# Beginning of a fused decoder step: input rows first, conditioning vectors and nine short rows on ScalarE's queue, the first conditioning weights ahead of two weight blocks

## What is computed

```python
mod = jax.nn.silu(c) @ w_ada + b_ada                       # c: 9 vectors, one for the prompt, 8 for the samples
sh1, sc1, g1, sh2, sc2, g2 = split(mod, 6)
h = rmsnorm(x, norm_mix_w) * (1.0 + sc1) + sh1
z = h @ w_in + b_in                                        # split into q, f, i, og, glu_a, glu_b, gate_a, gate_b
```

## Time and profile before

| | us |
|---|---|
| median of 3 runs | 1910.36 (1909.33 to 1912.45) |
| profiled execution, its own time | 1907.86 |
| its span in the profile | 1906.1 |
| TensorE busy | 1874.0, 98% of the span |
| VectorE / ScalarE / GpSimd busy | 1412.5 / 674.3 / 231.5 |

### The profile page before, as it was taken

How to read it: one execution, slowest core, us unless ns; L and a number is a source line. 1 busy time by engine, 2 the same in 40 slices (tenths; PEclk the granted TensorE clock), 3 DMA queues, 4 the chain that set the end, 5 groups by cost and what they waited for, 6 DMA issues and landing times.

```text
span 1906.1 us, 38795 instructions
## 1 busy us (share of the span) xinstructions
PE 1874.0 (98%) x15832; PEld 1820.0 (95%) x15832; DVE 1412.5 (74%) x2068; ACT 674.3 (35%) x1175; POOL 231.5 (12%) x301
## 2 busy tenths in 40 slices
PE   7999999999999999999999999999999999999998
PEld 6999999999999999998999999999999999999998
DVE  6797979787878888797676666566469988985653
ACT  4322313141322313232454433333445444443432
POOL 5500000000000000000002357476000000000000
PEclk8999999999999999999999999999999999999999
DMA  9722132323130413223277644554542333327653
GB/s 285 225 64 68 46 106 57 105 58 106 50 101 25 125 37 82 80 75 96 74 247 227 193 131 138 165 164 142 153 128 85 94 100 108 94 71 217 194 166 109
DMA packets 382010, 228.22 MB, mean 120 GB/s; under 512 B 17479, under 2 KB 375015, under 8 KB 381824
## 3 DMA queue, kind: packets, MB, share of 16 engines
q1 hardware_dynamic: 381424, 225.11, 40.3%
q10 hardware_dynamic: 416, 0.72, 0.1%
HBM read 195.69 MB, written 30.96 MB: 119 GB/s over the span
## 4 chain that ended last, share of the span: by engine, by line
PE 90%; DVE 5%; DMA 2%; ACT 1%; SPq 1%; issue 1%; POOL 0%; ACTq 0%; DVEq 0%; POOLq 0%
PE Z L1092 36%; PE Z L1074 28%; PE Z L1379 5%; PE Z L1380 5%; PE Z L1381 5%; PE R L1113 2%; DVE w_lo L1557 1%; PE Z L1037 1%; PE R L1169 1%; DMA w_raw<-in_w_out_dram 1%; PE R L1119 1%; ACT w_hi L2253 1%; PE R L1195 1%; PE R L1202 1%; PE R L1176 1%; PE R L1204 1%
## 5 line engine op out<-in xcount | busy, mean ns | idle before, releaser
L1092 PE MATMUL Z<-h_hi,w_hi 128*128 128x352 f32 x1488 | 499.2, 336 | 2.3 <-issue 2.3
L1092 PE MATMUL Z<-h_hi,w_lo 128*128 128x352 f32 x1488 | 478.1, 321 | 0.0
L1092 PE MATMUL Z<-h_lo,w_hi 128*128 128x352 f32 x1488 | 477.6, 321 | 0.0
L2253 ACT ACTIVATE w_hi<-w_raw 128x1024 fp32r<-128x1024 f32 (+1 forms) x227 | 235.0, 1035 | 673.4 <-PE Z L1092 360.8
L1557 DVE TENSOR_TENSOR w_lo<-w_raw,w_hi 128x1024 fp32r<-128x1024 f32 (+1 forms) x225 | 285.0, 1267 | 228.7 <-ACT w_hi L2253 220.0
L1706 DVE SCALAR_TENSOR_TENSOR yb<-up,vec,yb 128x1024 f32 (+1 forms) x240 | 308.3, 1285 | 28.9 <-DVE yb L1706 4.6
L1092 PEld LDWEIGHTS Z<-h_hi,w_hi 128*128 128x128 f32 x1488 | 279.5, 188 | 16.2 <-issue 14.1
L1092 PEld LDWEIGHTS Z<-h_lo,w_hi 128*128 128x128 f32 x1488 | 280.3, 188 | 0.5 <-issue 0.5
L1092 PEld LDWEIGHTS Z<-h_hi,w_lo 128*128 128x128 f32 x1488 | 279.2, 188 | 0.0
L1074 PE MATMUL Z<-act_hi,w_hi 128*128 128x352 f32 x528 | 171.8, 325 | 0.1
L1379 PE MATMUL Z<-h_hi,q_hi 128*128 128x352 f32 x528 | 171.0, 324 | 0.0
(11 more groups left out here) (365 smaller groups left out, 3422.0 us busy)
## 6 DMA issues: line engine op xcount, KB each, us to landing
w_raw<-in_w_in_dram SPq DMA_DIRECT2D x64, 512.0 KB, 5.9
w_raw<-in_w_out_dram SPq DMA_DIRECT2D x48, 512.0 KB, 4.3
w_raw<-in_w_ffn_out_dram SPq DMA_DIRECT2D x47, 512.0 KB, 4.3
w_raw<-in_w_ffn_in_dram SPq DMA_DIRECT2D x44, 512.0 KB, 3.8
raw_a<-in_w_ffn_in_dram SPq DMA_DIRECT2D x88, 256.0 KB, 2.9
aw<-in_w_ada_dram SPq DMA_DIRECT2D x32, 512.0 KB, 5.2
w_raw<-in_w_ffn_out_dram SPq DMA_DIRECT2D x24, 384.0 KB, 3.5
ada_w<-in_w_ada_dram SPq DMA_DIRECT2D x16, 512.0 KB, 7.1
```

The costliest lines, as they stand in the source:

```text
L1092: last = mm(out, w[:, kt, :], x[:, kt, cols], start=kt == 0 and m == 0, stop=kt == NJ - 1 and m == 2)
L2253: A(w_hi[b.par][:, 0:n, :], w_raw[b.par][:, 0:n, :], ACT.Copy).then_inc(w_hi_ready, 1)
```

## The change

SP issues all nine x tiles first, then three of the twelve short rows (norm_mix_w, b_ada, lb_logits), then w_ada for j = 0, the two weight blocks, and the rest of w_ada. The two DMAs of the conditioning vectors and the other nine short rows are issued by ScalarE, the nine one by one behind its nine Squares. The multiply of the conditioning vectors goes from VectorE to GpSimd; the low part of block 1 goes from GpSimd to VectorE, between `scale_prompt(0)` and `prompt_low(0)`; the low part of block 0 goes behind all reciprocal roots on GpSimd. The roots' rows are copied in three pieces of up to four tiles, in place of nine. `vectors()` goes behind the last root row, `conditioning(1)` stands right behind `fold_groups(0)`, `fold_groups(1)` is inside the first step, and the steps of the first products run through kt in order for both blocks to the end.

```diff
-FIRST_STEPS = tuple((kt, b) for kt in range(NJ - 2) for b in range(2)) + tuple(
-    (kt, b) for b in range(2) for kt in range(NJ - 2, NJ))
+FIRST_STEPS = tuple((kt, b) for kt in range(NJ) for b in range(2))
+COND_AFTER = {**{(kt, 0): kt + 2 for kt in range(NJ - 3)}, (NJ - 4, 1): NJ - 1}
+FOLD_WITHIN = {(0, 0): 1, **{(kt, 1): kt + 2 for kt in range(NJ - 3)}}
+FOLD_AFTER = {(NJ - 3, 0): NJ - 1}
+ROWS_A_BANK = 4
+N_ROW_COPIES = (NC + ROWS_A_BANK) // ROWS_A_BANK
...
-            sp.dma_start(crow[0:1, :], c_prompt).then_inc(c_loaded, 16)
-            sp.dma_start(crow[1:NSEQ, :], c_sample).then_inc(c_loaded, 16)
...
-            for t in range(4):
+            for t in range(NC + 1):
                 load_x(t)
...
+            load_rows(sp, V_MIX, 0, norm_mix_w[0].rearrange("(r c) -> r c", c=P))
+            load_rows(sp, 0, 1, b_ada[0].rearrange("(r c) -> r c", c=P))
+            load_rows(sp, V_LB0 - NVA, 1, lb_logits.rearrange("l (r c) -> (l r) c", c=P))
...
-            for t in range(4, 6):
-                load_x(t)
+            load_mod(0)
             for b in range(2):
                 load_first(b)
-            for t in range(6, NC + 1):
-                load_x(t)
-            for j in range(NJ):
+            for j in range(1, NJ):
                 load_mod(j)
...
-                    if t == 2:
-                        vectors()
+                    if t == 4:
+                        conditions()
                 for t in range(NC - 1, NC + 1):
                     root_row(t)
+                vectors()
                 pe.wait_ge(const_ready, 3)
-                for j in range(2):
-                    conditioning(j)
-                    fold_groups(j)
+                conditioning(0)
+                fold_groups(0)
+                conditioning(1)
...
-                        if b == 1 and m == 1 and kt + 2 < NJ:
-                            fold_groups(kt + 2)
+                        if m == 1 and (kt, b) in FOLD_WITHIN:
+                            fold_groups(FOLD_WITHIN[kt, b])
                     if kt == NJ - 1:
                         last.then_inc(block_done, 1)
-                    if b == 0 and kt + 2 < NJ:
-                        conditioning(kt + 2)
+                    if (kt, b) in FOLD_AFTER:
+                        fold_groups(FOLD_AFTER[kt, b])
+                    if (kt, b) in COND_AFTER:
+                        conditioning(COND_AFTER[kt, b])
...
             for j in range(NJ):
                 condition(j)
                 scale_prompt(j)
+                if j == 0:
+                    dve.wait_ge(w_split, 1)
+                    low(Idx(1))
                 prompt_low(j)
...
+            act.dma_start(crow[0:1, :], c_prompt).then_inc(c_loaded, 16)
+            act.dma_start(crow[1:NSEQ, :], c_sample).then_inc(c_loaded, 16)
             act.wait_ge(c_loaded, 32)
...
-
-                if t == 5:
-                    for b in range(2):
-                        hi(Idx(b))
+                load_rows(act, *late_rows[t])
             groups_out(0)
+            for b in range(2):
+                hi(Idx(b))
...
+            pool.wait_ge(c_loaded, 32)
+            pool.wait_ge(csig_ready, 1)
+            st.tell(Q.tensor_tensor(crow[:, :], crow[:, :], csig[:, :], ALU.mult), c_ready, 1)
             for t in range(NC + 1):
                 m = tokens(t)
-                if t == 6:
-                    for b in range(2):
-                        low(Idx(b))
...
+            low(Idx(0))
```

More of the change, by code:

```diff
@@ L545, in store_last, with load_rows @@
             eng.dma_start(y_sample.rearrange("s t d -> (s t) d")[:, cols], yout(c)[n:m, cols]).then_inc(y_stored[hf], 16)
+    def load_rows(eng, row, tile, src):
+        eng.dma_start(vrow[row:row + src.shape[0], tile, :], src).then_inc(rows_loaded, 16)
     def rec7(n):
@@ L958, in _, with conditions @@
             pe.wait_ge(const_ready, 2)
[L960 to L963, removed]
+            def conditions():
+                pe.wait_ge(c_ready, 1)
+                for j in range(NJ):
+                    last = transpose(R[0][:, j * NSEQ:(j + 1) * NSEQ], crow[:, j * P:(j + 1) * P], ident[0:NSEQ, 0:NSEQ])
+                last.then_inc(p0_done, 1)
             def vectors():
@@ L1499, in lower_bounds, with copy_rows @@
                 st.do(V.tensor_scalar(lbs[:, 2, :], lbs[:, 0, :], 1.0, None, ALU.subtract))
-            def copy_row(t):
-                dve.wait_ge(row_made, t + 1)
-                st.tell(V.tensor_copy(rsrow[:, t * P:t * P + tokens(t)], row_bank(t)), row_copied, t + 1)
+            def copy_rows(n):
+                first, end = n * ROWS_A_BANK, min((n + 1) * ROWS_A_BANK, NC + 1)
+                cols = sum(tokens(t) for t in range(first, end))
+                dve.wait_ge(row_made, end)
+                st.tell(V.tensor_copy(rsrow[:, first * P:first * P + cols], Z[1][:, n, 0:cols]), row_copied, n + 1)
             def condition(j):
@@ L1520, in _ @@
                         "p (j t) -> p j t", j=4)), x_evac, n + 1)
-                if t >= 2:
-                    copy_row(t - 2)
-                if t == 3:
-                    first_evac(1, vec[:, :], R[1][:, 0:NVEC])
-            for t in range(NC - 1, NC + 1):
-                copy_row(t)
+                if t == 5:
+                    first_evac(0, ct[:, :, 0:NSEQ], R[0][:, 0:NJ * NSEQ].rearrange("p (j s) -> p j s", s=NSEQ))
+                if t == 6:
+                    copy_rows(0)
+            for n in range(1, N_ROW_COPIES):
+                copy_rows(n)
+            first_evac(1, vec[:, :], R[1][:, 0:NVEC])
             def scale_prompt(j):
@@ L1540, in prompt_low, with low @@
                     st.do(ins) if n == 0 else st.tell(ins, h_ready, j + 1)
+            def low(b, n=8):
+                dve.wait_ge(w_hi_ready, b.v + 1)
+                st.tell(V.tensor_tensor(w_lo[b.par][:, 0:n, :], w_raw[b.par][:, 0:n, :],
+                                        w_hi[b.par][:, 0:n, :].bitcast(F32), ALU.subtract), w_split, b.v + 1)
             for j in range(NJ):
```

33 lines of the change are left out of this document (10 added, 23 removed).

## The result

| | before | after |
|---|---|---|
| median in the same comparison, 12 runs each | 1910.07 (1908.06 to 1912.51) | 1913.92 (1910.12 to 1918.02) |
| ratio to before, 95% interval | | 1.0023 [1.0016, 1.0030] |
| profiled execution, its own time | 1907.86 | 1917.03 |
| its span | 1906.1 | 1915.3 |
| first 352-column matmul, T0 | 32.40 | 36.15 |

The change makes the kernel slower by 3.85 us, 0.23%. That lies above the range given. By the rivals, the time sits between the third and the fourth, and the mechanism is the fourth's.

A forecast was written before the change was run, and what follows sets the result against it. TensorE, 90% of the last-ending chain, was taken as the bound, its head held back by the DMA stream. First 352-column matmul -1.3, from there to block 2 +0.6: -0.7 from 1910.36 gives 1909.7 us, range 1905.6 to 1912.9.

The forecast's parts named there:

- the third: Rival 3, chance 0.15: row issues on ScalarE stand between the Squares, first 352-column matmul at 33.6, +1.8 us, 1912.2.
- the fourth: Rival, chance 0.08: last short row waits behind SP's queued megabytes, lands at 25.9, first 352-column matmul 37.7, +5.9, 1916.3.
- The landing of the last short row: Last row on ScalarE's queue: issued at 16.3, landing taken as 3.0 us, short rows complete at 19.3 (17.6 to 26).
- From the landing to the copy-out: Transposes, copy and conditioning(0) after the short rows: 1.6 + 1.5 + 0.7 for the low clock, copy-out's end at 23.1.
- From the copy-out to T0: Rounding, GpSimd's low part, xs and samples(0): 6.8 us plus 1.2 for VectorE's subtraction, 8.0, ending at 31.1.
- held up by it: scale_prompt operations on VectorE could delay, or be delayed by, GpSimd's low part of block 0; delaying it: up to 1.5 later.
- The sign it gave for GpSimd: On GpSimd's timeline, xs or a first sample operation takes about 1.2 us longer than before.
- Issues on ScalarE: Nine row issues of 0.3 to 0.6 us run during the Squares and cost nothing; ninth Square begins at 15.7.
- From T0 to B2: First 352-column matmul to start of block 2, the steady part: 37.6 us before, small parts together +0.6.
- The wait of 1.65: TensorE's wait at 65.57 for VectorE's last h_lo goes; the copy-out before fold 7 may hold 0.3: -1.35.
- The new wait at B2: Start of block 2: both first blocks now end together, so TensorE waits 2.6 - 1.46 = +1.15 us.
- -2.7 and +1: Ends for the clock between first 352-column matmul and block 2: taken as 0; -2.7 if high all the way.

## Why the prediction was wrong

- **The landing of the last short row.** The step that failed is the one that took 3.0 us for it, "nearer to the small transfer: it is 62 KB, on a queue that has nothing else". It took 6.72, from 16.82 (forecast 16.3). The bounds, 1.93 and 9.6, held it. The choice between them went by size, where the load at the time of issue should have decided: the 1.93 us had been measured ahead of x, when nothing else was in flight, and the 9.6 us under the load that the last row would meet. The c vectors show this inside the changed kernel, 3.8 in place of 1.93. The transposes came at 23.58 in place of 19.4, +4.2 us of the 5.05 by which T0 was missed (36.15 against 31.1). With it T0 came after the 33.5 that the prediction had set as its own limit. The move of the nine rows to SP gave back 3.3 us against the kernel before (4.2 by the bare medians).
- **From the landing to the copy-out.** Forecast 3.8 us, measured 23.54 to 28.11, 4.6. I had counted half the price of the low clock on this piece; it was low all along: +0.8.
- **From the copy-out to T0.** Forecast 8.0, measured 8.0, but along another way. I had GpSimd's chain last, and made it 1.2 longer by VectorE's subtraction. In fact VectorE was held up by GpSimd, 2.08 in place of 0.29, and its own subtraction (1.26) then came last with `h_lo`. The prediction named this case, "held up by it", for the operations of `scale_prompt`, and left it out of the sum. The sign it gave for GpSimd, an operation 1.2 us longer, came at 0.5 (1.22 in place of 0.70). With the low part earlier on GpSimd T0 moved by 2.24.
- **Issues on ScalarE.** Right: they cost the Squares nothing, the ninth was at 16.77 (forecast 15.7) because the last full tile of x landed later, with a wait of 0.83 for it, not because of the issues. The first Square, at 6.12 (forecast 4.49), stood behind the sigmoid, which waited 2.15 us for the c vectors; with the wait for x behind it, this cost nothing in the end. Rival 3's mechanism fell. At the start of the queue, where no work covers them, nine issues did cost 1.8 us.
- **From T0 to B2.** Forecast 38.2, measured 38.54. The wait of 1.65 went, without the 0.3 that I had kept of it. The new wait at B2 is 1.10 (forecast 1.15). `fold_groups(2)` does not wait, as said for the low clock; the sum had kept 0.5 for it. The clock was taken as unchanged; the low stretch behind T0 was 7.65 us against 5.6 before, half of the difference being 1.0. These make +1.2 with the 0.7 of `fold_groups(1)` at the low clock, 0.3 more than the 0.9 measured; the rest of the small parts isn't resolved.
- **The clock.** The end for it was "-2.7 and +1", and it came out at +1. I had argued that the idle time ahead of T0 would be as long as before; it was longer (4.32 and 5.10 us at a time), in one low stretch of 24 us. Kept at full speed, the changed kernel gained 3.0 us of median and 4.65 at B2.
- **Span and median.** B2 moved by 4.65 us and the medians of one comparison by 3.85. The profile of before has a mean clock of 0.996, where its timed runs have 0.995 in the mean; those at 0.996 took some 1908.7 us, those at 0.994 some 1910.6. So its B2 is probably an early one, which no second profile shows. I had used it as it stood.
- **The rivals.** The fourth had the mechanism, a small transfer behind SP's megabytes, at a chance of 0.08. Its price was 6.6 us of extra landing time and it was 3.7. It was said to decide once the row lands later than 23.8; 23.54 was enough, with the 0.8 that the clock added on the way. Against it I had put that the row has a queue of its own, and a rule on the order of packets that no row supported. The full DMA share of the earlier trace rows was the evidence, and it spoke for this rival.

## What to carry to other kernels

A small transfer issued late into a full DMA stream took 5.3 to 6.7 us here, on a queue of its own; the same rows issued early, on ScalarE's queue or on SP's, were not waited for. So what everything waits for goes out before the large loads, and a price for it is taken from a transfer that met the same load. When slack of ten microseconds is used up by a move, all that stood under its cover (here two roundings and two low parts) becomes part of the path, and where two engines exclude each other, the price has to be worked out in both directions. A gain at the head has to be checked in the median: of 3.3 us at block 2 none could be told at the end (ratio 1.0001, interval 0.9991 to 1.0010).

## What the runs showed of the hardware

- A row of 62 KB on ScalarE's queue, issued at 16.82, landed after 6.72 us, one of 32 KB, issued at 17.80, after 5.33: at nearly the same moment, 23.54 and 23.13. In the first case ScalarE's queue moved no packet from 18.5 to 20 us and 256 from 20 to 23, beside 1389 of SP's.
- A DMA issue on ScalarE takes 0.26 to 0.55 us and runs beside a Square of 1.06 without delaying it; nine of them ahead of all work put the first Square 1.8 us later.
- A TENSOR_SCALAR of 128 x 9 on VectorE took 2.08 us beside a TENSOR_TENSOR of 128 x 1024 on GpSimd, 0.29 without it. Two operations of 128 x 512 took 3.85 in place of 1.49 in the kernel with the rows at the start, where GpSimd's low part ran at the same time:

```profile
24.73 0.29 DVE L1506 TENSOR_SCALAR am<-mod,ones,vec 128x9 f32<-128x9 f32 x1
25.05 3.85 DVE L1525 SCALAR_TENSOR_TENSOR ta<-xt,am,rsrow 128x512 f32<-128x512 f32 x2
```

- The multiply of 9 x 1024 took 2.36 us on GpSimd, beside VectorE's copies, and 1.21 on VectorE.
- Identity matmuls of 128 x 128 in float32, 0.23 us each, held the clock at 1.00 through the head of all four kernels that had them.
